# A delta-rule inverse from four 32x32 diagonal blocks instead of two 64x64 ones, with projection steps between its levels

## What is computed

```python
n_mat = jnp.where(strict, -jnp.einsum('nbhid,nbhjd->nbhij', kb, kc) * decay, 0.0)
t_mat = jnp.eye(CHUNK, dtype=f32) + n_mat
p_mat = n_mat
for _ in range(int(math.log2(CHUNK)) - 1):
    p_mat = jnp.einsum('nbhij,nbhjk->nbhik', p_mat, p_mat)
    t_mat = t_mat + jnp.einsum('nbhij,nbhjk->nbhik', t_mat, p_mat)
u = jnp.einsum('nbhij,nbhjd->nbhid', t_mat, vb)
```

## Time and profile before

| | us |
|---|---|
| median of 3 runs | 2709.22 |
| lowest, highest | 2707.76, 2709.7 |
| the profiled execution: whole | 2707.76 |
| the profiled execution: span from first to last instruction | 2706.0 |

### The profile page before, as it was taken

The page is one execution under the profiler, slowest core; times in us unless marked ns, Lnnn a source line. Parts: engine busy times, 40 slices in busy tenths (PEclk is TensorE's granted clock), DMA queues, the critical chain, the costliest instruction groups (busy, mean ns, idle before and its releaser), DMA issues.

```text
span 2706.0 us, 50329 instructions
## 1 busy us (share of the span) xinstructions
PE 2682.5 (99%) x19808; PEld 2274.0 (84%) x19808; DVE 1416.5 (52%) x3633; ACT 971.0 (36%) x3158; POOL 398.7 (15%) x238
## 2 busy tenths in 40 slices
PE   7999999999999999999999999999999999999998
PEld 6888888888888888888888888888888888888887
DVE  6777777233366666612236666651224666665012
ACT  4555455422244444421124444442112444444101
POOL 4333333443100110000000110000000011000000
PEclk9999999999999999999999999999999999999999
DMA  7554554787733333255453333335546333333564
GB/s 249 201 180 167 182 193 170 264 288 279 253 121 111 128 128 117 107 203 217 172 219 130 112 114 125 130 110 203 216 172 220 113 118 128 123 112 125 183 222 171
DMA packets 79001, 458.43 MB, mean 169 GB/s; under 512 B 13232, under 2 KB 17456, under 8 KB 31792
## 3 DMA queue, kind: packets, MB, share of 16 engines
q1 hardware_dynamic: 65664, 427.85, 44.2%
q10 hardware_dynamic: 13104, 27.36, 3.0%
HBM read 352.42 MB, written 102.76 MB: 168 GB/s over the span
## 4 chain that ended last, share of the span: by engine, by line
PE 96%; DMA 2%; POOL 1%; DVE 1%; ACT 0%; issue 0%; POOLq 0%; SPq 0%; ACTq 0%; DVEq 0%
PE bank L1305 24%; PE bank L1307 23%; PE bank L1306 23%; PE bank L1450 2%; PE last_banks L1450 2%; PE last_banks L1415 2%; PE bank L1434 2%; PE last_banks L1434 2%; PE bank L1403 2%; PE bank L1499 1%; PE bank L1491 1%; PE bank L1475 1%; PE last_banks L1557 1%; PE bank L1483 1%; PE bank L1548 1%; PE bank L1538 1%
## 5 line engine op out<-in xcount | busy, mean ns | idle before, releaser
L1305 PE MATMUL bank<-hT_hi,w_sl 128*128 128x512 f32 x2112 | 872.8, 413 | 0.0
L1307 PE MATMUL bank<-hT_hi,w_sl 128*128 128x512 f32 x2112 | 827.3, 392 | 0.0
L1306 PE MATMUL bank<-hT_lo,w_sl 128*128 128x512 f32 x2112 | 825.5, 391 | 0.0
L1307 PEld LDWEIGHTS bank<-hT_hi,w_sl 128*128 128x128 f32 x2112 | 396.7, 188 | 86.1
L1305 PEld LDWEIGHTS bank<-hT_hi,w_sl 128*128 128x128 f32 x2112 | 398.3, 189 | 71.6 <-issue 0.7
L1306 PEld LDWEIGHTS bank<-hT_lo,w_sl 128*128 128x128 f32 x2112 | 398.8, 189 | 65.4 <-issue 0.7
L436 POOL TENSOR_TENSOR w_sl<-w_raw,w_sl 128x1024 fp32r<-128x1024 f32 x90 | 218.3, 2430 | 391.2 <-ACT w_sl L517 381.6
L982 DVE SCALAR_TENSOR_TENSOR area<-zraw,stc,area 128x512 f32<-128x512 f32 x288 | 220.2, 765 | 4.2
L1148 DVE SCALAR_TENSOR_TENSOR s_cur<-s_cur,scs,last_banks 128x128 f32<-128x128 f32 x112 | 38.9, 348 | 199.8 <-PE last_banks L1554 199.8
L611 ACT ACTIVATE area<-area 128x512 f32<-128x512 f32 x96 | 60.4, 629 | 219.6 <-DVE area L982 219.6
L455 POOL TENSOR_TENSOR gu<-mk,g_hi 128x512 fp32r<-128x512 f32 x32 | 41.9, 1309 | 643.7 <-DVE nmx L1102 603.8
(11 more groups left out here) (244 smaller groups left out, 4817.7 us busy)
## 6 DMA issues: line engine op xcount, KB each, us to landing
w_sl<-saved_w SPq DMA_DIRECT2D x270, 1024.0 KB, 4.8
saved_w<-w_sl SPq DMA_DIRECT2D x90, 1024.0 KB, 4.9
w_raw<-in_w_tiles SPq DMA_DIRECT2D x90, 512.0 KB, 5.9
area<-in_x ACTq DMA_DIRECT2D x4, 2048.0 KB, 10.4
area<-in_x ACTq DMA_DIRECT2D x14, 512.0 KB, 8.1
out_y<-area ACTq DMA_DIRECT2D x3, 2048.0 KB, 8.1
bias_sb<-in_bias ACTq DMA_DIRECT2D x32, 128.0 KB, 2.3
out_y<-area SPq DMA_DIRECT2D x4, 512.0 KB, 2.7
```

The lines of the kernel that those rows point to most:

```text
L1305: pe.matmul(dst, a_hi, b_hi, start=first, stop=False)
L1306: pe.matmul(dst, a_hi, b_lo, start=False, stop=False)
L1307: return pe.matmul(dst, a_lo, b_hi, start=False, stop=last)
```

## The change

It replaces the two 64x64 diagonal blocks by four of 32x32 (`BLOCKS`), for which four levels do, and one further `apply`. Two 64x64 inverses then come from four 32x32 ones by two new products, `inner_in` and `inner_out`, over the corners in between (`CORNERS`), and the merge to 128x128 follows as it was.

- PE: each `square` and `apply` has 8 matmuls of 32 rows in the place of 4 of 64 rows. The second part of `apply` has 32 columns, so it writes 64 in all, not 128. `fill(11)` becomes `fill(8)`; one `fill(1)` stands behind each of the levels 2, 3 and 4; the `fill(2)` behind the last `apply` becomes three of `fill(1)`, behind it and behind either new product. The last `apply` writes both groups to one bank.
- DVE: the first powers come from a DVE transpose (`first_powers`, between `logits(0)` and `attention`) rather than from ACT's copies of PE's transpose, and the identity is added to them there and no longer ahead of the logits. `settled` is gone. `diagonal` adds four blocks of 32 partitions, then transposes two of them for `inner_in`; `inner_corners` copies what `inner_out` made.
- ACT: two of three copies at L710 go (the one for `od` stays); the first layout is in four copies of 32 partitions, not two of 64; a copy `yt` stands between the two new products.

```diff
-LEVELS = 5
+BL = 32
+LEVELS = 4
+        BLOCKS = tuple(slice(r, r + BL) for r in range(0, P, BL))
+        CORNERS = ((BLOCKS[0], BLOCKS[1]), (BLOCKS[2], BLOCKS[3]))
...
-                act.wait_ge(ssq_ready[0], n1)
                 act.wait_ge(ft_done, n1)
-                for lo, hi in HALVES:
-                    act.activation(p_sb[0][lo:hi], bch(5)[lo:hi, :, lo:hi], ACT.Copy)
-                act.activation(od[CH:P], bch(5)[CH:P, :, 0:CH], ACT.Copy).then_inc(p0_ready, 1)
+                act.activation(od[CH:P], bch(5)[CH:P, :, 0:CH], ACT.Copy).then_inc(merge_act, 1)
...
+                act.wait_ge(merge_product, merges(n1, 1))
+                act.activation(yt, bch(5)[:, :, 0:BL], ACT.Copy).then_inc(merge_act, 1)
...
-                for lo, hi in HALVES:
-                    ins = dve.tensor_tensor(ptt[lo:hi, :, CH:P], tt[lo:hi, :, lo:hi],
-                                            mk[lo:hi, IDENT:IDENT + 1, lo:hi].to_broadcast([CH, NT, CH]), ALU.add)
-                ins.then_inc(tt0_ready, 1)
...
+                def first_powers():
+                    dve.wait_ge(pt0_ready, n1)
+                    dve.wait_ge(ssq_ready[0], n1)
+                    dve.transpose(p_sb[0][:, :, 0:BL], ptt[:, :, 0:BL]).then_inc(p0_ready, 1)
+                    dve.tensor_tensor(ptt[:, :, BL:2 * BL], ptt[:, :, 0:BL],
+                                      stacked[:, None, :].to_broadcast([P, NT, BL]), ALU.add).then_inc(tt0_ready, 1)
...
+                def diagonal():
                     for g in range(2):
                         dve.wait_ge(tt_ready[g], n1 * (LEVELS - 1))
+                        dve.wait_ge(a_done[g], n6 + (LEVELS + 1))
+                    for i in (0, 2, 1, 3):
+                        r = BLOCKS[i]
+                        ins = dve.tensor_tensor(tt[r, :, r], bch(A_BANK[0])[r, :, BL:2 * BL], ptt[r, :, BL:2 * BL], ALU.add)
+                        if i in (0, 2):
+                            ch.inc(ins)
+                    ins.then_inc(diag_ready, 1)
                     ch.sync()
+                    for a, _ in CORNERS:
+                        ins = dve.transpose(vt[a], tt[a, :, a])
+                    ins.then_inc(merge_dve, 1)
+
+                def inner_corners():
+                    dve.wait_ge(merge_product, merges(n1, 2))
+                    for a, c in CORNERS:
+                        ins = copy(tt[a, :, c], bch(7)[a, :, 0:BL])
+                    ins.then_inc(merge_dve, 1)
...
                     for t in (2 * g, 2 * g + 1):
-                        for lo, hi in HALVES:
-                            ins = pe.matmul(pv(bank[P_BANK[g]])[lo:hi, t, 0:width], ptt[lo:hi, t, 0:CH], p_sb[(l - 1) % 2][lo:hi, t, 0:width], start=True, stop=True)
+                        for r in BLOCKS:
+                            ins = pe.matmul(pv(bank[P_BANK[g]])[r, t, 0:BL], ptt[r, t, 0:BL], p_sb[(l - 1) % 2][r, t, 0:BL], start=True, stop=True)
...
+                def inner_in():
+
+                    pe.wait_ge(merge_dve, merges(n1, 1))
+                    for t in range(NT):
+                        for a, c in CORNERS:
+                            ins = pe.matmul(bch(5)[c, t, 0:BL], tt[a, t, c], vt[a, t, :], start=True, stop=True)
+                    ins.then_inc(merge_product, 1)
+
+                def inner_out():
+
+                    pe.wait_ge(merge_act, merges(n1, 2))
+                    pe.wait_ge(diag_ready, n1)
+                    for t in range(NT):
+                        for a, c in CORNERS:
+                            ins = pe.matmul(bch(7)[a, t, 0:BL], yt[c, t, :], tt[c, t, c], start=True, stop=True)
+                    ins.then_inc(merge_product, 1)
...
-                fill(11)
+                fill(8)
                 probs(0)
                 for l in range(1, LEVELS + 1):
                     square(l, 0)
...
                     if l == 1:
                         logits_quarters(0)
+                    else:
+                        fill(1)
                 logits_quarters(1)
                 apply(LEVELS + 1, 0)
                 apply(LEVELS + 1, 1)
-                fill(2)
+                fill(1)
+                inner_in()
+                fill(1)
+                inner_out()
+                fill(1)
                 merge_in()
```

More of the change, by code:

```diff
@@ L89, in state_steps, with merges @@
     return (n1 - 1) * NT + t + 1 - max(0, n1 - 1 - (NB - 1) * H)
+def merges(n1, step):
+    return (n1 - 1) * 3 + step
 class Chain:
@@ L1116, in head @@
                 logits(0)
+                first_powers()
                 attention()
```

74 lines of the change are left out of this document (30 added, 44 removed).

## The result

| | median us | runs | ratio to before, 95% |
|---|---|---|---|
| before | 2709.2 | 2707.8 to 2709.7 | |
| after | 2788.6 | 2786.7 to 2793.1 | 1.0296 (1.0278 to 1.0314) |

The change costs 79 us. The forecast said 42 us in the same direction; 2788.6 lies inside its range. The profiled execution of the changed kernel took 2789.2 us, with a span of 2787.3 us.

A forecast was written before the change was run, and what follows sets the result against it. PE was taken to bound the kernel. Per head -1.11 + 1.0 + 0.93 = +0.82, 26 us in 32 heads, plus 12 + 3.5 behind `probs(0)`, made +42: 2707.8 + 42 + 1.5 = 2751 us, range 2693 to 2797.

The forecast's parts named there:

- PE's own streaming, -1.11 us a head: PE's inverse up to the merge, shape changes included, takes 7.27 us a head instead of 8.38: 1.11 saved.
- feeding, +1.0: Bringing matmuls up from PE's queue at 35 ns each adds 1.0 us a head, bounds 0 and 2.4.
- streaming 0.12: A 32x32 group of 16 records on PE takes 0.12 us if streaming sets its pace.
- feeding 0.28: A 32x32 group of 16 records on PE takes 0.28 us if bringing up its matmuls sets the pace.
- Shape changes, 0.37 a round trip: PE leaving the tiled shape and returning costs 0.37 us; six trips a head instead of one, 2.22 us.
- The three changes between 64 and 32: PE switching between 64x64 and 32x32 tiles around the logits drains the engine: 0.15 us each, 0.45 a head.
- DVE's chain, "a new wait of 0.93 us a head": Behind level 5, PE waits 0.93 us before `inner_in` for DVE's four additions and two transposes; bounds 0.3 and 1.4.
- Behind `probs(0)`, 12 and 3.5 us: With three fills fewer ahead, PE waits for DVE's quotient: 12 us mostly in the first block, 3.5 over 23 heads.
- the 0.65 that an earlier ACT was to give back: In first-block heads, ACT done 0.77 us earlier lets GpSimd's split start earlier, cutting the wait by 0.65.
- whatever changes PE's own queue changes the time one for one: Starting step: PE is busy 99% of the span, so other engines' waits count only where PE stands behind them.
- nothing is queued ahead: Rival, chance 0.10: all matmuls come at 35 ns, feeding costs 2.4 us a head instead of 1.0; 2797 us.
- The rival with a floor of 25 ns a record: Chance 0.03: PE records start at least 25 ns apart, 8.0 us a head instead of 3.14; 2860 us.

The follow-up runs named there:

- run with the steps alone: Kernel before (blocks of 64) with only the moved steps: 8 instead of 11 ahead of the inverse, one behind levels 2, 3 and 4 each; 2756.4 us.
- run with the corner first: Changed kernel with DVE adding blocks 0 and 2, then making their transposes, and adding blocks 1 and 3 only afterwards; 2756.9 us.
- the seven heads without a hole above: Later heads of the changed kernel with blocks 0 and 2 first on DVE and, in blocks two to four, three steps behind level 3, two behind level 5; 2719.2 us.
- two runs with 51 and 70 us of holes: Changed kernel with 11 steps ahead, none behind levels 2 to 4: 2839.5 us; changed kernel with 32 more matmuls at PE's start: 2893.8 us, one run.
- a third with 42: Changed kernel with 11 steps ahead, the steps behind levels 2, 3 and 4 kept, and 46 matmuls at PE's start; 2854.4 us.
- one with 38 us of holes and the short chain: Changed kernel with blocks 0 and 2 first on DVE, 10 steps ahead and one step between the levels, behind level 3 alone; 2746.1 us.

## Why the prediction came out as it did

Taken by its own steps:

- **PE's own streaming, -1.11 us a head, and feeding, +1.0.** The kind is right for the first. Sixteen records take 0.15 where "streaming 0.12" and "feeding 0.28" were the two poles, also in the groups that open a level. 14 groups at 0.15, 4 at 0.23 and the two new products at about 0.26 (two tiles at a time, last record 0.25 after the first, alike behind the wait and without one) are 3.5 us against the 4.1 that 3.14 + 1.0 gave. In an undisturbed head (the thirteenth) PE's own time is 12.79 less six steps (4.10) less the wait of 1.24: 7.45 us against 8.38 before. So 0.93 is saved where -1.11 + 1.0 gave 0.11. What the earlier trace rows showed for one pair of loads behind a wait was not the price of all matmuls. The feeding term was the one mis-sized most.
- **Shape changes, 0.37 a round trip.** The run with the steps alone gives 0.26 with blocks of 64. In the changed kernel three trips cost 0.25 net, with the replies that they cover; of the 7.45 some 2.05 are left for all six, 0.34 each. The three changes between 64 and 32 that were taken at 0.45 by the rule of the tiling mode are seen: in the same head 0.12, 0.20 and 0.20 us lie between the last record of one shape and the first of the other, where 0.01 and 0.055 are usual, 0.40 in all. No run isolates them.
- **DVE's chain, "a new wait of 0.93 us a head".** Right in kind, 1.24 in size, within the bounds 0.3 to 1.4. The additions of 32 partitions run one after the other, 0.305 each; they don't overlap, as those of 64 partitions didn't in the earlier trace rows. The transposes were priced at 0.23 from copies and take 0.305. The run with the corner first halves this wait, and the time follows.
- **Behind `probs(0)`, 12 and 3.5 us.** 15.3 measured, of which 14.3 in the first block: 1.9 us a head where 1.2 was taken, so the 0.65 that an earlier ACT was to give back didn't come; in the later blocks it is 1 us instead of 5.5. The run with the steps alone has the same wait, so it is the steps and hardly `first_powers`.
- **The sum.** The listed terms gave +42 and measured 25. The direction was right for the reasons given, but 54 of the 79 us come from two things that the list didn't have. That 2788.6 lies in the range is luck: the range went up to 2797 for a feeding term that the rows refute, and the same program shifted by 128 instructions is far outside it. The step that failed stands at the very start: "whatever changes PE's own queue changes the time one for one" was worked out by durations alone. It counted PE's instructions by their duration and never by their number.
- **The rival "nothing is queued ahead" (2797 us)** is nearest in time and wrong in mechanism: behind a wait the groups stream. The rival with a floor of 25 ns a record is out: 16 records in 0.15 us are 9 ns each. (Its time, by the forecast's own terms, should have been 2874 and not 2860: 2751 + 32 x (8.0 - 3.14 - 1.0).)

**Instruction fetch.** The order had shown the additional matmuls, and the page the count of instruction packets; counting would have shown 256 instructions passing in well under the 4.8 us that was the shortest before (1.9 to 3.5 in front of the holes). The runs show what it meets. From one boundary to the end of a hole at the next it is 3.1 to 4.5 us in the changed kernel, and 4.8 to 5.9 where the boundary before had a hole too; over all runs 2.9 to 7.1. (The expectations speak of 3.4 at least; single crossings are shorter.) The Trainium skill, "Runtime: NRT & Kernel Launch", section "Instruction fetch mechanics", says that each engine is refilled in blocks of 256 instructions while it runs the current one, and that crossing a boundary is "mostly hidden". The packets of this trace agree on the 256. On "hidden" the measurement decides: with 256 instructions in 4.8 us or more it nearly always is (three holes of 0.5 to 0.9 us in the two traces with blocks of 64 and the steps where they were), and with four small tiles running side by side it isn't.

**Why the small blocks still lose at their best.** The inverse with its steps has 736 instructions in the changed kernel, before 424. At 3.4 us for 256, a short crossing, that is 9.8 us, as much as the whole section took before. This is an estimate. What speaks for it are the seven heads without a hole above, which are faster than before: what four tiles save in streaming counts where other work stretches the boundaries apart.

**What stays open.** Which idle time brings the lower clock: two runs with 51 and 70 us of holes and DVE's long chain have 220 us of it, a third with 42 only 101, one with 38 us of holes and the short chain only 20, the run with the steps alone had it behind single waits of 1.9 us and no hole, and the same instructions had it in one execution and not in another. So the 33 us in the account are put down to the clock, but no run takes them away alone. That a boundary after a fast one takes 5 us and more is shown (packets start 4.6 to 5.0 us apart there in the changed kernel, up to 6.5 in the shifted one), but not why. Gaps under half a microsecond at the boundaries aren't counted anywhere.

## What to carry to other kernels

Count instructions as well as time: where a change cuts an engine's work into more and shorter pieces, divide the time of the fastest section by its packets of 256 and compare it with the shortest stretch in the profile that runs without a hole. If a kernel's time jumps by per cents for a few instructions added far away, as here by 105 us for 128, number the records, semaphore instructions with them, and look whether the gaps stand at one remainder. When a step of cover work is moved ahead or between, follow it to the place that it leaves: here a head's projection steps were all spoken for.

## What the runs showed of the hardware that was not expected

- PE's instructions come in packets of 16 KB, 256 at a time; in the runs with blocks of 32 PE stood at 15 to 45 boundaries of 196 until 2.2 to 3.6 us after a packet's start, mostly when the 256 before had passed in 1.8 to 3.5 us (up to 5 where the ones before those had been fast too); some boundaries were passed as fast without standing.
- The same program, shifted by 128 instructions, took 2894 (one run) instead of 2789 us; with blocks of 64 the same shift changed 2709 to 2713.
- PE's granted clock was 0.5 in stretches of 3.4 to 13.7 us, where ahead of them PE had idled 1 to 2 us in or before a tiled section (two holes and a wait in the head shown above, a single wait of 1.9 in the run with the steps alone), but not each time. A fully busy record then takes 0.43 us instead of 0.228.
- DVE's operations on 32 partitions x 128 elements run at 0.305 us each one behind the other, additions and transposes alike, as long as those on 128 partitions (0.29).
